# Token tile by token tile at the four norms between a two-layer transformer's units, on one core

## The reference

```python
for i in range(DEPTH):
    h = rmsnorm(x, g[0])
    mix = swa_sink_attention(h, ...) if i % 2 == 0 else nsa_attention(h, ...)
    x = x + rmsnorm(mix, g[1])
    h = rmsnorm(x, g[2])
    x = x + rmsnorm(conv_ffn(h, ...), g[3])
return x
```

## Time and profile before

| what | us |
|---|---|
| median of 3 runs | 2125.11 |
| lowest, highest | 2124.90, 2125.21 |
| the profiled execution's own time | 2124.99 |
| its span, first to last instruction | 2123.3 |
| PE busy | 2111.3 (99%) |
| DVE busy | 1335.1 (63%) |
| ACT busy | 1064.3 (50%) |
| POOL busy | 277.6 (13%) |

### The profile page before, as it was taken

How to read it: one execution, slowest core, us unless ns; L and a number is a source line. 1 busy time by engine, 2 the same in 40 slices (tenths; PEclk the granted TensorE clock), 3 DMA queues, 4 the chain that set the end, 5 groups by cost and what they waited for, 6 DMA issues and landing times.

```text
span 2123.3 us, 34632 instructions
## 1 busy us (share of the span) xinstructions
PE 2111.3 (99%) x12195; PEld 1808.7 (85%) x12195; DVE 1335.1 (63%) x2031; ACT 1064.3 (50%) x1620; POOL 277.6 (13%) x461
## 2 busy tenths in 40 slices
PE   9999999999999999999999999999999999999999
PEld 9987788888888888888999977888888888888887
DVE  7665676766767754445866664676766767754444
ACT  6675554444444444444656775554444444444443
POOL 4452000000000000001205763000000000000000
PEclk9999999999999999999999999999999999999999
DMA  7444555565565565555673333556555565565553
GB/s 255 150 162 156 169 177 198 179 193 182 178 200 185 185 211 189 188 188 169 217 249 113 106 114 120 168 177 196 180 191 185 177 200 186 182 214 189 188 189 129
DMA packets 107505, 381.42 MB, mean 180 GB/s; under 512 B 14147, under 2 KB 14867, under 8 KB 106771
## 3 DMA queue, kind: packets, MB, share of 16 engines
q1 hardware_dynamic: 105106, 373.63, 53.7%
q10 hardware_dynamic: 2304, 6.53, 0.9%
HBM read 377.97 MB, written 2.14 MB: 179 GB/s over the span
## 4 chain that ended last, share of the span: by engine, by line
PE 98%; DVE 1%; POOL 0%; issue 0%; ACT 0%; DMA 0%; DVEq 0%; ACTq 0%; POOLq 0%
PE set L733 32%; PE set L826 31%; PE set L737 16%; PE set L951 11%; PE set L1025 1%; PE set L999 1%; PE set L1047 1%; PE set L877 1%; PE set L1001 0%; PE set L1049 0%; DVE x_sb L1920 0%; PE set L1115 0%; PE set L1116 0%; POOL probs L671 0%; PE set L1058 0%
## 5 line engine op out<-in xcount | busy, mean ns | idle before, releaser
L1732 DVE TENSOR_TENSOR wlo<-raw,whi 128x1024 fp32r<-128x1024 f32 x703 | 860.4, 1233 | 572.8 <-ACT whi L1285 570.5
L1285 ACT ACTIVATE whi<-raw 128x1024 fp32r<-128x1024 f32 x703 | 737.3, 1056 | 731.2 <-PE set L737 350.6
L733 PE MATMUL set<-hs,whi 128*128 128x512 f32 x2932 | 966.3, 395 | 0.9 <-ACT whi L1381 0.9
L737 PE MATMUL set<-hs,wlo 128*128 128x256 f32 x2944 | 695.5, 281 | 0.0
L737 PEld LDWEIGHTS set<-hs,wlo 128*128 128x128 f32 x2944 | 544.7, 188 | 60.6
L733 PEld LDWEIGHTS set<-hs,whi 128*128 128x128 f32 x2932 | 503.3, 189 | 71.0 <-DVE hs L1822 1.1
L826 PE MATMUL set<-whi,hid 128*128 128x512 f32 x1408 | 388.7, 395 | 0.0
L826 PEld LDWEIGHTS set<-whi,hid 128*128 128x128 f32 x1408 | 264.2, 188 | 64.2 <-DVE wlo L1732 0.6
L826 PE MATMUL set<-wlo,hid 128*128 128x512 f32 x704 | 223.6, 395 | 0.0
L951 PE MATMUL set<-hs,whi 128*128 128x256 f32 x1280 | 213.1, 286 | 0.0
L951 PEld LDWEIGHTS set<-hs,whi 128*128 128x128 f32 x1280 | 176.7, 189 | 2.3 <-issue 0.4
(11 more groups left out here) (208 smaller groups left out, 1346.7 us busy)
## 6 DMA issues: line engine op xcount, KB each, us to landing
raw<-in_stream SPq DMA_DIRECT2D x703, 512.0 KB, 3.5
gain_rows<-rows ACTq DMA_DIRECT2D x4, 1024.0 KB, 5.3
xT<-in_x SPq DMA_DIRECT2D x8, 256.0 KB, 7.7
out_y<-out_f SPq DMA_DIRECT2D x3, 512.0 KB, 3.0
bo_rows<-rows ACTq DMA_DIRECT2D x1, 1024.0 KB, 12.7
wg_raw<-in_w_gates ACTq DMA_DIRECT2D x1, 768.0 KB, 5.2
raw<-in_stream SPq DMA_DIRECT2D x2, 256.0 KB, 4.1
w2k_sb<-in_w ACTq DMA_DIRECT2D x2, 128.0 KB, 7.5
```

The source lines that it names most:

```text
L733: return mm(sets[set_of(u)][:, t, 0:2 * w], whi[:, slot, cols], r, start=first, stop=final)
L737: return mm(sets[set_of(u)][:, t, w:2 * w], wlo[:, slot, cols], r[:, 0:w], start=False, stop=False)
L1285: A(whi[:, slot, :], raw[:, slot, :], ACT.Copy).then_inc(hi_ready, 1)
L1732: V.tensor_tensor(wlo[:, slot, :], raw[:, slot, :], whi[:, slot, :].bitcast(F32), ALU.subtract).then_inc(lo_ready, 1)
```

## The change

The diff touches all four norms.

- **The last unit before a norm.** PE keeps the last three chunks together (`HELD = 3`) and does all 18 products of token tile 0, then all 18 of tile 1. Near the end of tile 1's products it turns the first two column chunks of tile 0 (`between`).
- **The first unit after a norm.** `first_chunks` takes the place of the first two chunks of `unit`. Column chunks 0 and 1 of x are taken in parts of 128 columns and one token tile (`PARTS`): `turn_part`, `high_of_part`, `low_of_part`. The high products of chunk 0 and most of chunk 1 run for the first tile's tokens, then for the second's (each 2 x 128 columns: high and low part of `hs`), and the low products of the weights last. `keep_busy` is gone.
- **ACT and DVE around it.** Two splits of weights (the next unit's chunks 1 and 2) move from ahead of the norm into it; the tile 1 squares stand behind the first tile's high parts. The adds of x go one column chunk at a time and later in the unit.
- **The end.** Tile 0's x is added and turned while tile 1's products run. Six column chunks of tile 1 (`SUMMED_BANKS = 3` banks of four 128-column pieces) are summed on PE. The output is stored in eight pieces, each one token tile of four 128-column pieces (rows of 512 B in place of 1 to 4 KB).

```diff
-TURNED_SUMS = 2
+SUMMED_BANKS = 3
-IDLE_PRODUCTS = (4, 3)
+PARTS = [(0, 0), (0, 1), (1, 0), (1, 1)]
+HELD = 3
-OUT_PARTS = [(0, 4, 2), (4, 8, 4), (8, 12, 6), (12, 14, 7), (14, 15, 8), (15, 16, 9)]
+OUT_PARTS = [(0, 0), (0, 1), (0, 2), (0, 3), (1, 0), (1, 1), (1, 2), (1, 3)]
...
+            def last_chunks(u, k, source, n, between):
+                for t in range(TT):
+                    for c in range(n - HELD, n):
+                        g = first_chunk(u) + c
+                        if t == 0:
+                            pe.wait_ge(lo_ready, g + 1)
+                        for j in range(CK):
+                            between(t, c - n, j)
...
+                        if t == 0 and c == n - 1:
+                            ins.then_inc(y_first, 1)
+                        if t == 1:
+                            ins.then_inc(chunk_used, 1)
...
+                first_tokens((0, 1, 2))
+                if n < 3:
+                    first_tokens((3,))
+                turn_part(n, 0, 1)
+                for j in range(CK):
+                    pe.wait_ge(h_part, part_count(n, 0, j, 1))
+                    for tile in range(UT):
+                        if n == 3 and (j, tile) == (0, 3):
+                            first_tokens((3,))
+                        high(0, j, tile, 1)
+                    if j == 0:
+                        turn_part(n, 1, 1)
+                pe.wait_ge(lo_ready, g + 1)
...
             def prenorm(n, gain, u):
 
                 g0 = first_chunk(u)
-                for c in range(CH):
+                split(g0 + 1)
+                for c, kt in PARTS[:3]:
+                    high_of_part(n, gain, c, kt, 0)
+                if n > 1:
+                    high_of_part(n, gain, 1, 1, 0)
+                y_evac(u - 1, n - 1, 3, (1,))()
...
+                for c, kt in PARTS:
+                    high_of_part(n, gain, c, kt, 1)
+                split(g0 + 2)
+                for c in range(CK, CH):
                     high_of_h(n, gain, c)
-                    if 1 <= c <= 5:
-                        split(g0 + c + RING - 2)
-                    if 2 <= c <= 5:
+                    if c <= 6:
+                        split(g0 + c + 1)
+                    if c <= 5:
                         square_x(n, c - 2)
                     if c == 6:
                         take_root(n)
...
+                split(g0 + 1)
+                low_of_h(n + 1, gain, 2)
...
+                add_y(3, 4, x_ready, 1, (1,))
+                split(g0 + 2)
+                low_of_h(n + 1, gain, 3)
+                add_y(4, 5, x_ready, 1)
                 split(g0 + 3)
-                low_of_h(n + 1, gain, 2)
-                add_y(4, 6, x_ready, 2)
+                add_y(5, 6, x_ready, 1)
+                low_of_h(n + 1, gain, 4)
                 split(g0 + 4)
-                low_of_h(n + 1, gain, 3)
-                add_y(6, 8, x_ready, 2)
+                add_y(6, 7, x_ready, 1)
+                low_of_h(n + 1, gain, 5)
                 split(g0 + 5)
-                low_of_h(n + 1, gain, 4)
+                add_y(7, 8, x_ready, 1)
+                low_of_h(n + 1, gain, 6)
                 split(g0 + 6)
-                low_of_h(n + 1, gain, 5)
+                token_sum(sq_x, x_squared, 8 * (n + 2))
                 split(g0 + 7)
-                token_sum(sq_x, x_squared, 8 * (n + 2))
-                low_of_h(n + 1, gain, 6)
...
+            last_bank(0, 2)
+            for b in range(SUMMED_BANKS):
+                if b == 2:
+                    pe.wait_ge(out_ready, 1)
+                for n, (c, f, at) in enumerate(bank_tiles(b)):
+                    mm(out_bank(1, b)[:, at], x_sb[:, c, 1, f], ident[:], start=n == 0, stop=False)
+            last_bank(0, 3)
+            pe.wait_ge(diag_part, 1)
+            for b in range(SUMMED_BANKS):
+                for n, (c, f, at) in enumerate(bank_tiles(b)):
+                    ins = mm(out_bank(1, b)[:, at], y[:, c, 1, f], diag[:, 1, :], start=False, stop=n == 2 * CK - 1)
+                ins.then_inc(out_turned, 1)
+            pe.wait_ge(out_ready, 2)
+            last_bank(1, 3)
```

More of the change, by code:

```diff
@@ L737, in low @@
                         return mm(sets[set_of(u)][:, t, w:2 * w], wlo[:, slot, cols], r[:, 0:w], start=False, stop=False)
[L739 to L753, removed]
                     if u == KV0 and j == 0 and c < last_c:
@@ L789, in chunk, with unit @@
                 last.then_inc(chunk_used, 1)
-            def unit(u, source, lp=None, width=S, waits=None, tile_before=None, after_chunk=None, spread=0, low_ready=0):
+            def unit(u, source, lp=None, width=S, waits=None, tile_before=None, after_chunk=None, spread=0, done=0):
                 n = CH
@@ L796, in unit @@
                 at = None if v is None else more_e + (UT * v + 1)
-                for c in range(n):
+                for c in range(done, n):
                     g0 = first_chunk(u) + c
@@ L830, in token_chunk, with token_unit @@
                 ins.then_inc(chunk_used, 1)
-            def token_unit(u, k, source, waits=None):
-                for c in range(CHF if source is hid else CH):
+            def token_unit(u, k, source, waits=None, between=None):
+                n = CHF if source is hid else CH
+                for c in range(n - HELD if between else n):
                     if waits:
@@ L1214, in _ @@
                 else:
-                    turn_x(n, 0)
-                    unit(KC1, hs, waits=h_waits(n), tile_before=mid_chunk(n), low_ready=n)
+                    first_chunks(n, KC1)
+                    unit(KC1, hs, waits=h_waits(n), done=CK)
                     spread_r(n)
@@ L1233, in _ @@
                 output_pair(o0, o_waits, attention(layer, GROUPS - 1))
+                n = 2 * layer + 1
                 for k in range(2, 4):
-                    token_unit(o0 + k, k, os_)
-                n = 2 * layer + 1
-                turn_x(n, 0)
-                unit(ff, hs, waits=h_waits(n), tile_before=mid_chunk(n), low_ready=n)
+                    token_unit(o0 + k, k, os_, between=between_norm(n) if k == 3 else None)
+                first_chunks(n, ff)
+                unit(ff, hs, waits=h_waits(n), done=CK)
                 spread_r(n)
@@ L1311, in unit @@
                 last = u == UNITS - 1
-                for c in range(done, n + (0 if last else RING - 1)):
+                for c in range(done, n + (0 if last else 1 if norm_next else RING - 1)):
                     split(g0 + c, more, turn)
@@ L1899, in evac @@
                 def evac():
+                    if k == 3:
+                        return
                     if k == 0:
```

355 lines of the change are left out of this document (219 added, 136 removed).

## The result

The changed kernel takes 2131.67 us (median of 8 runs, 2130.44 to 2132.34), the kernel before beside it 2125.2 us; the ratio is 1.0034, with a 95% interval of 1.0025 to 1.0043. It is slower, by 6.5 us by the medians and 7.2 us by the ratio. The profiled execution took 2131.59 us, its span is 2129.8 against 2123.3 us.

The account below looks back on a forecast made before the run. The prediction took PE as the bound, its chain of waits lying there for 98% of the span. 2125.1 + 4.75 (norms) + 0 (end) = 2129.9 us, plus 0.7 for the clock: 2130.6 us, range 2122.5 to 2134.5.

Parts of the forecast that it names:

- The first tile's products begin at once, the second tile's chain stays: Next unit's start: first tile's products fill 1.4 to 1.9 us of PE's idle time, then PE waits for tile 1.
- Chunk 6: Chunk 6 of the unit after each inner norm: PE was to wait 1.85 us there, in each of three units.
- the ring: Before chunk 6: ACT's high part, squares and DVE's add, split, low part wait on each other; 8.2 us against PE's 6.3.
- Norms: The three inner norms: losses of 1.2, 1.4 and 1.85 us, 0.3 more at the second for POOL; 4.75 us slower.
- The end, 0: Program end: no net change, bounds -0.5 and +0.7 us; PE's additional products offset early turns, last stores land as before.
- The clock: PE's granted clock after the norms' waits: 0.7 us added for a possible fall to 0.50.
- whether one of them costs a fall is even: At the norms: even chance that one of the three 1.85 us waits makes PE's clock fall; 0.7 us taken.
- no second new fall: Answers the rival that PE's clock falls twice or more behind the norms' waits: 2133.3 to 2135 us, chance 0.18.
- chunk 6 did wait: Answers the rival that PE does not wait at chunk 6 after the inner norms: 2124.4 us, chance 0.17.
- the second tile was waited for: Answers the rival that the new unit runs on without tile 1's waits: 2119.4 us, chance 0.10.
- the splits behind the norm delayed nothing at the start: Answers the rival that moved splits delay the first tile's products, some 1.5 us a norm: 2134 us, chance 0.05.

Follow-up runs that it names:

- e1: Changed kernel with DVE's add of x's column chunk 7 moved ahead of the low part of column chunk 5: 2126.03 us, ratio 1.0006 to the kernel before.
- e2: Changed kernel with ACT squaring x's columns 6 and 7 behind the high part of column chunk 6 instead of ahead: 2126.41 us, ratio 1.0008 to the kernel before.
- e3: Changed kernel plus eight unread identity products in PE's waits at the first norm alone: 2129.81 us, ratio 1.0028 to the kernel before.
- e8: Kernel before without its unread products at the three inner norms: 2125.19 us, ratio 1.0003 to the kernel before.
- e10: Changed kernel with DVE's splits of weight chunks 1 to 7 behind each inner norm cut to 64 of 1024 columns: 2121.82 us, ratio 0.9984.
- e4: Changed kernel with PE adding the last sum into two banks of the second tile, not three; DVE adds the third's x: 2130.48 us, ratio 1.0027.
- e6: e5 with DVE adding x's column chunk 3 of the second tile before the low part of column chunk 2: 2123.81 us, ratio 0.9999.
- e9: Kernel before with only its end replaced, by that of e4; the three inner norms unchanged: 2123.94 us, ratio 0.9996.
- e5: Changed kernel with the edits of e2, e3 and e4 together: 2123.32 us, ratio 0.9994 to the kernel before.
- e7: Changed kernel with PE holding back the second tile's products of one chunk, not three, in each last unit: 2142.49 us, ratio 1.0085.

## Why the prediction was right

It forecast 2130.6 us, slower, for the reasons that the traces then showed; by its own steps:

- *The first tile's products begin at once, the second tile's chain stays*: so. The waits at the first norm were put at 0.5, 0.8 and 1.35 us; from start to start they are 0.5, 0.9 and 1.3. A product of 2 x 128 columns in place of 256 costs nothing more: sixteen of L963 take 2.06 us behind the second norm, their starts 0.119 apart, as in the earlier trace rows.
- *Chunk 6*: the ring was summed to 8.2 us and took 8.0 (from 268.37, where the turns end, to 276.36); PE was there after 6.4, where 6.3 was said; it waited 1.6 us in place of 1.85. Between ACT and DVE a hand-over took 0.03 to 0.04 us, as taken, and from the split's end to PE 0.14; what was shorter are the low parts, 0.79 us to the next start on DVE where 0.93 was taken. e1 and e2 show that this ring was the cause.
- *Norms*: 1.2, 1.7 (with POOL) and 1.85 us were forecast without the clock. Norm 1 at full clock (e3) is 1.31 above the kernel before, norms 2 and 3 are 1.72 and 1.81 above it. Sum 4.84 against 4.75. That it is met to 0.1 us is in part luck: the ring alone was put 0.25 us too high at each norm, and terms put too low made up for it, of which one is known (at the second norm the split of chunk 2 is waited for 1.0 us from start to start, where 0.7 was said).
- *The end, 0*: 0.04, within what the span is given to. The last product's start to PE's end was put at 7.0 us and is 6.9 (2118.82 to 2125.76, four turns behind 2125.29). Eight products more on PE eat what the first tile's early turns bring, and the stores moved at the rate that was taken.
- *The clock*: the one term that was mis-sized. 0.7 us stood for an even chance of one fall of 1.7. The profile has that fall at the first norm, and it costs 1.45, which is 0.75 of the 1.07 us by which the median lies above the forecast. It is also likelier than even: 7 of 8 runs have two falls or more, where the kernel before has 6 of 75. The step that failed is "whether one of them costs a fall is even": the earlier trace rows showed a wait of 1.50 us without a fall, and the unread products beside it were held for a small matter. e8 shows that in the kernel before they kept the clock up; in the changed kernel e3 brings it back with them, and e1 and e10 show that they are not the only thing that counts.
- The rivals: the profile has no second new fall, chunk 6 did wait, the second tile was waited for, and the splits behind the norm delayed nothing at the start (the first product follows after 0.25 us).

## What to carry to other kernels

Starting the next stage on half of the data hides the chain of that half alone; the other half's chain is as long as before and needs as much work beside it, so count that work first. When a hand-over is split, look for the steps that ran ahead before (here the adds, two column chunks early): giving up their lead can close a ring over three engines in which each waits and none is busy, and the cure is an order, not speed. Unread products in a wait look like waste and may not be, if the engine's clock depends on them: read the granted clock of many runs with and without them, and the time too, since a fall in a stretch that waits anyway costs little (e8).

## What the runs showed of the hardware

- The clock's falls are a matter of chance for the same program. PE's wait of 1.89 us for POOL stands in every profile; behind it the granted clock over 1290 to 1304 us is 0.88 in the kernel before, the changed one, e2, e4, e6 and e9, and 1.00 in e1, e3, e5, e8 and e10; e7, 10 us later there, has the fall too (0.68 over 1304 to 1308). The Trainium skill, "TensorE: Matmul & The Clock Gate", section "What's actually happening", has it that the monitor's timing does not start with the kernel, so that the same kernel is slowed differently from run to run; the runs of the kernel before agree (30 at 1.000, 39 at 0.999, 6 at 0.998). What else decides, no run here tells.
- A fall cost between 0.47 us (e8, norm 2) and 1.6 us. The latter is the one behind PE's wait for POOL: from the product after that wait to the third norm's mark it is 101.26 us in the kernel before and 99.69 in e8, which lacks the fall, and 102.96 in the changed kernel and 101.36 in e3, which lacks it.
- Rows of 512 B are stored at 258 to 298 GB/s where the stores run without a gap, longer ones (864 packets for 2.1 MB in place of 4224) at 340 to 445. The kernel before over 2110 to 2124 us and the changed one over 2112 to 2130, in 40 slices each:

```profile
GB/s 0 0 0 0 0 0 0 0 0 0 0 0 0 0 0 0 0 0 0 12 433 398 421 398 386 398 445 386 421 398 386 340 380 345 337 108 0 0 0 0
```

```profile
GB/s 0 0 0 0 0 0 0 0 0 0 0 0 0 0 0 118 290 174 264 289 30 118 290 174 0 0 0 149 282 272 286 288 289 258 273 298 291 227 0 0
```

The prediction had only a read to go by the earlier trace rows; for stores the two lines above show the same. They decide against the 512 B that the Trainium skill, "DMA: Bandwidth & Descriptors", Specifications, gives as enough for line rate.
